# First mixer of a two-layer encoder trunk: k and v by features, recurrence laid between projection blocks, output projection in plain fp32

## The chip, the cores and the metric

The kernel runs on one core of a Trainium2 chip, as one launch. The metric is device microseconds of that launch. Engines are named as in the profile: PE is the matrix engine, DVE the vector engine, ACT the scalar engine, POOL is GpSimd, SP issues most of the DMAs. Each engine works through its own instructions in the order written; semaphores are the only links between them.

## What is computed

Two layers over 272 tokens (16 meta tokens and 256 real ones) of width 1024, all inputs fp32. The first layer's mixer, which the change rebuilds, is this, cut to what matters:

```python
def conv_gla_mixer(h, w_in, conv_w, wg_f, bg_f, wg_b, bg_b, gla_norm_w, w_out):
    u = h @ w_in
    a_b, a_c, a_x, q, k, v, r, g_f, g_b = jnp.split(u, splits, axis=-1)   # 512 x3, 256 x2, 512 x2, 16 x2
    y_a = a_b * centred_depthwise_conv3(a_c * a_x, conv_w)
    log_a_f = jax.nn.log_sigmoid((g_f @ wg_f + bg_f)) / GLA_GATE_TAU       # log_a_b likewise
    o_fwd = gla_chunked(qh, kh, vh, laf, True)                             # chunks of 64 tokens, 4 heads
    o_bwd = flip(gla_chunked(flip(qh), flip(kh), flip(vh), flip(lab), False))
    o = rms_norm per head (o_fwd + o_bwd) * gla_norm_w
    y_b = (o * jax.nn.silu(r))
    return jnp.concatenate([y_a, y_b], axis=-1) @ w_out

# gla_chunked, per chunk and head:
    scores = q*exp(cum) . k*exp(-cum), masked;  o_intra = scores @ v
    kv_chunk = (k*exp(cum_last - cum))^T @ v;  S = exp(cum_last) * S + kv_chunk;  o_inter = q*exp(cum) @ S_before
```

Behind the mixer stands a mixture of 32 experts with two chosen per token; then a second layer with grouped-query attention and experts of its own, then a final norm.

## The kernel before

Everything is written by hand, engine by engine, in one function; what the code says is the order, and no scheduler moves it. Three tiles hold the tokens: tile 0 has the 16 meta tokens, tiles 1 and 2 have 128 each (`TILE_AT`, `TILE_N`). `B[0]` to `B[7]` are the eight PSUM banks. `slots` are the 16 ring slots of 1 MB; the mixer's weights go through slots 0 to 7 (`MIX_RING`), and `scratch`, the mixer's working memory, lies over slots 8 to 15, so that expert weights can land there only when the mixer has done with it. The profile calls `scratch` whatever is carved out of it.

**Split products.** The mixer's projections are exact to fp32 by three products. A block `b` of 512 columns of weights comes in two units `u = 2b` and `2b+1`, for the features 0 to 3 and 4 to 7 of every eight. ACT rounds a unit into one of three buffers `mix_hi` (`round_mix`, L546); then DVE or POOL subtracts and writes the rest, `mix_lo`, in place (`low_mix`, L280; `MIX_POOL` says which units POOL takes). The features have the same two parts, `hnT_hi` and `hnT_lo`. PE then makes three passes for each product (`split_product`, L1331 to L1333): high by high, and twice high by low. Unit `u` can be rounded when unit `u-3` has been read; `mix_used` says that a block's first unit is read, `proj_ps` that a block's piece is finished. `feature_major` puts features on the rows and all 272 tokens in the columns; `token_major` puts a tile's tokens on the rows and 512 weight columns (256 for k) in the columns.

**Order on PE.** Gate ranks g; q feature-major, k token-major; the gate product (L1375); v token-major; six transposes that turn k (L1384); r token-major; conv block ax feature-major; the cumulated log decays (L1402) and end decays (L1410, L1411); conv blocks ac and ab. Then the recurrence: chunk sums (L1432, `chunk_sums`), scores (L1445), outputs from scores (L1460) and from states (L1473), transposes of the result yb (L1481), and the output projection, blocks 6 and 7, split and token-major, 144 passes. DVE does the decays, the conv taps (L913, L915), `ya` (L920), then the states: each of eight steps takes four pieces of 64 rows and 128 columns (L935, L937), then masks (L945), head norms (L958). The result becomes high and low parts again: ACT rounds ya (L611) and yb (L628), POOL and DVE write the low parts (L434, L964).

**Behind it.** DVE adds the projection to h (L990) tile by tile and norms tiles 0 and 1 in between (L816). PE transposes h (L1520) and makes the routing products. Experts go in quads: gather (L1608), gate and up products in four column strips of 32 rows (L1577), down (L1595), scatter (L1633). SP issues the expert weights: units 0 and 1 when block ac is read, 2 and 3 when ab is, 8 to 15 when yb is transposed and `pool_step` and `feat_hi` say that the scratch is free, 4 to 7 when the output weights are read (`first_units0`), and each further group of four when the stage that used its slots is done (`rest_of_units`). The second layer's projection back (L1798) is in plain fp32 with its features `hnT` and ring slots as they landed.

## Time and profile before

| | us |
|---|---|
| median of 3 runs | 828.09 (827.14 to 828.76) |
| the profiled execution | 826.41 |
| its span, first to last instruction | 824.6 |
| PE busy | 669.4 (81%) |
| DVE busy | 271.3 (33%) |
| ACT busy | 182.3 (22%) |
| POOL busy | 73.2 (9%) |
| bytes moved by DMA | 234.86 MB |

The profile is of one execution. A row of a line groups all instructions with that line, engine and shape: count, busy time together, mean time of one, and the engine's idle time before them with what ended it. On PE the mean is the time from start to end of one pass, and passes overlap; the rate is the stretch divided by the count. A plain fp32 product is recorded as two passes, a split product's passes as one each. PEclk is the granted clock as a share of 2.4 GHz: 1.00 or 0.50 at any moment, and a mean over a stretch.

### The profile page before, as it was taken

The numbers are of one execution on the slowest core, as the hardware profiler recorded it, in microseconds if no ns is written. First come the engines' busy times: TensorE is split into PE (matmuls) and PEld (weight loads), VectorE is DVE, ScalarE is ACT, GpSimd is POOL, SyncE is SP. The second block draws the span as 40 slices with busy tenths as digits, with TensorE's granted clock in tenths as the row PEclk, the third lists the DMA queues.
The fourth block names the chain that finished last, engine by engine and source line by source line (L and its number), as shares of the span: only waits on it lengthen the run. The fifth ranks groups of instructions, "written<-read, shape, count | busy, mean of one in ns | idle before, by whom it ended". The sixth has DMA issues, their size and how long they took to land.

```text
span 824.6 us, 9320 instructions
## 1 busy us (share of the span) xinstructions
PE 669.4 (81%) x3824; PEld 379.9 (46%) x3824; DVE 271.3 (33%) x608; ACT 182.3 (22%) x347; POOL 73.2 (9%) x47
## 2 busy tenths in 40 slices
PE   2999987896999679679678987899797668678665
PEld 2867986576727126226214665545535215215211
DVE  4242346335322212221214777612422202202204
ACT  4394513212101001000004426712111001001002
POOL 3223209300000000000004200000000000000000
PEclk9999997998999989979879999999799869869869
DMA  9534433783399999999998332059299999999991
GB/s 309 216 106 155 148 103 106 233 324 118 105 415 400 403 417 413 410 416 406 407 409 297 103 128 78 1 198 385 83 388 395 415 405 411 414 415 406 414 384 53
DMA packets 62164, 234.86 MB, mean 285 GB/s; under 512 B 6256, under 2 KB 6512, under 8 KB 53920
## 3 DMA queue, kind: packets, MB, share of 16 engines
q1 hardware_dynamic: 60848, 231.82, 72.5%
q0 software_dynamic: 1264, 2.34, 1.2%
q8 instruction: 34, 0.56, 0.3%
q14 instruction: 18, 0.15, 0.1%
HBM read 233.07 MB, written 1.05 MB: 284 GB/s over the span
## 4 chain that ended last, share of the span: by engine, by line
PE 50%; DMA 18%; SPq 13%; DVE 10%; ACT 5%; issue 3%; DVEq 0%; ACTq 0%
DMA ring<-in_moe_w_up 17%; SPq L329 13%; PE bank L1577 10%; PE bank L1608 7%; PE bank L1331 5%; PE bank L1332 5%; PE bank L1333 5%; PE bank L1633 4%; PE bank L1798 3%; PE bank L1595 3%; ACT scratch L759 2%; DVE mix_lo L280 1%; ACT mix_hi L546 1%; DVE scratch L1263 1%; DMA gain<-in_norm_mix 1%
## 5 line engine op out<-in xcount | busy, mean ns | idle before, releaser
L1577 PE MATMUL bank<-ring,hnT 128*32 128x512 f32 x1024 | 150.5, 743 | 83.5 <-DMA ring<-in_moe_w_up 80.0
L1577 PEld LDWEIGHTS bank<-ring,hnT 128*32 128x32 f32 x1024 | 38.4, 132 | 191.7 <-issue 119.1
L1608 PE MATMUL bank<-sel,hn 128*128 128x256 f32 x320 | 82.9, 419 | 0.3 <-DVE sel L1056 0.3
L1608 PEld LDWEIGHTS bank<-sel,hn 128*128 128x128 f32 x320 | 79.2, 336 | 3.5 <-issue 1.7
L280 POOL TENSOR_TENSOR mix_lo<-ring,mix_hi 128x2048 fp32r<-128x2048 f32 x11 | 51.9, 4727 | 315.4 <-ACT mix_hi L546 315.4
L1633 PE MATMUL bank<-moe_scratch 128*128 128x512 f32 (+1 forms) x160 | 78.1, 611 | 1.8 <-ACT moe_scratch L669 1.6
L1118 DVE TENSOR_TENSOR moe_scratch<-moe_scratch,bank 128x256 f32<-128x256 f32 x16 | 6.7, 421 | 215.9 <-ACT moe_scratch L663 215.9
L1331 PE MATMUL bank<-mix_hi,hnT_hi 128*128 128x512 f32 (+3 forms) x168 | 65.2, 388 | 3.9 <-DVE mix_lo L280 2.2
L1332 PE MATMUL bank<-mix_hi,hnT_lo 128*128 128x512 f32 (+3 forms) x168 | 64.8, 386 | 0.0
L1333 PE MATMUL bank<-mix_lo,hnT_hi 128*128 128x512 f32 (+3 forms) x168 | 64.6, 385 | 0.0
L1108 DVE TENSOR_TENSOR h<-bank,h 128x512 f32<-128x512 f32 (+1 forms) x80 | 55.1, 689 | 23.6 <-PE bank L1633 23.6
L1595 PE MATMUL bank<-ring,moe_scratch 128*32 128x512 f32 x512 | 58.2, 595 | 0.3 <-ACT moe_scratch L665 0.3
L663 ACT ACTIVATE moe_scratch<-bank 128x256 f32<-128x256 f32 x16 | 6.1, 383 | 216.2 <-PE bank L1577 216.2
L546 ACT ACTIVATE mix_hi<-ring 128x2048 fp32r<-128x2048 f32 x22 | 41.3, 1908 | 35.4 <-PE bank L1333 35.0
L1633 PEld LDWEIGHTS bank<-moe_scratch 128*128 128x128 f32 (+1 forms) x160 | 22.7, 169 | 55.3 <-issue 32.6
L280 DVE TENSOR_TENSOR mix_lo<-ring,mix_hi 128x2048 fp32r<-128x2048 f32 x11 | 27.8, 2539 | 30.7 <-ACT mix_hi L546 30.7
L1331 PEld LDWEIGHTS bank<-mix_hi,hnT_hi 128*128 128x128 f32 (+1 forms) x168 | 28.4, 169 | 17.8 <-issue 4.1
L1099 DVE COPY hnT<-bank 128x512 f32<-128x512 f32 x16 | 11.1, 692 | 76.6 <-PE bank L1608 76.6
L1331 PE MATMUL bank<-hnT_hi,mix_hi 128*128 128x272 f32 x112 | 32.7, 292 | 2.6 <-DVE mix_lo L280 1.8
L1333 PEld LDWEIGHTS bank<-mix_lo,hnT_hi 128*128 128x128 f32 (+1 forms) x168 | 28.2, 168 | 9.9 <-issue 0.6
L1332 PEld LDWEIGHTS bank<-mix_hi,hnT_lo 128*128 128x128 f32 (+1 forms) x168 | 28.4, 169 | 9.2 <-issue 0.8
L1332 PE MATMUL bank<-hnT_hi,mix_lo 128*128 128x272 f32 x112 | 32.3, 288 | 0.0
(262 smaller groups left out, 734.5 us busy)
## 6 DMA issues: line engine op xcount, KB each, us to landing
ring<-in_moe_w_gate SPq DMA_DIRECT2D x128, 512.0 KB, 14.3
ring<-in_moe_w_up SPq DMA_DIRECT2D x128, 512.0 KB, 14.5
ring<-in_moe_w_down SPq DMA_DIRECT2D x64, 1024.0 KB, 17.0
ring<-in_sc_w_in SPq DMA_DIRECT2D x12, 1024.0 KB, 12.5
ring<-in_att_w_in SPq DMA_DIRECT2D x6, 1024.0 KB, 15.3
ring<-in_sc_w_out SPq DMA_DIRECT2D x4, 1024.0 KB, 6.3
ring<-in_att_w_out SPq DMA_DIRECT2D x4, 1024.0 KB, 10.8
h<-in_x SPq DMA_DIRECT2D x2, 512.0 KB, 4.1
```

The lines of the kernel that those rows point to most:

```text
L280: ops.tensor_tensor(mix_lo[slot][:, :], slots[slot], mix_buf(u)[:, :].bitcast(f32), ALU.subtract)\
L329: sp.dma_start(gu[:, u], src).then_inc(sem(f"weights{l}_{stage_of(i) % 4}"), 16)
L546: nc.scalar.activation(mix_buf(u)[:, :], slots[at[-1]], ACT.Copy).then_inc(sem("mix_hi"), 1)
L1108: nc.vector.tensor_tensor(hh, B[[7, 4][k % 2]][0:n, :], hh, ALU.add).then_inc(sem(f"h_added{l}"), 1)
L1331: mm(dst, left[0], right[0], start=start, stop=False)
L1332: mm(dst, left[1], right[0], start=False, stop=False)
L1333: return mm(dst, left[0], right[1], start=False, stop=stop)
L1577: last = mm(B[2][at, :], xT[:, c, mine], w[j][:, :, cc, :], start=(c == 0), stop=(c == KC - 1))
L1595: last = mm(B[5 + half][at, :], heT[:, c, at], w[j][:, c * D + half * W:c * D + half * W + W], start=(c == 0), stop=(c == 1))
L1608: last = mm(B[k % 2][:, 2 * P * cc:2 * P * cc + 2 * P], hn[:, t, c:D:KC], picks, start=(t == a), stop=(t == b - 1))
L1633: mm(B[[7, 4][k % 2]][0:m, :], selgT[:, TILE_AT[t]:TILE_AT[t] + m], y[:, half, :], start=True, stop=True).then_inc(sem(f"sc_ps{l}"), 1)
L1798: last = mm(B[2 * half + i][:, :], hnT[:, c, i * P:(i + 1) * P], slots[u % MIX_RING][:, c % 4 * W:c % 4 * W + W], start=(c == 0), stop=(c ...
```

## The change

- **k and v** become feature-major. k's two blocks go straight to `kT`, and six transposes give the token-major `ktok`. v's four blocks go to `vT`, twelve transposes give `v`. Both lie in memory that `masked` takes later.
- **log decays**: ACT does Abs for three tiles, Exp for three, Ln for three, in place of all three functions for each tile in turn.
- **the last two pieces of a block** are made as a pair (`feature_pair`): first unit for both, then second unit for both.
- **order**: log and end decays come ahead of r; then one r tile, four chunk sums, the second r tile, four chunk sums, the third r tile, scores, ax, scores, ax pair, outputs, scores, ac, outputs, ac, outputs, ac pair, ab, yb transposes, ab pair, yb transposes.
- **states** are kept on 128 rows: a chunk sum makes four products of 64 rows each in place of two of 128, and DVE updates both heads of a pair in one instruction.
- **the output projection** is in plain fp32 from `hnT` and the ring slots: tiles 1 and 2 as whole products, the meta tile for both halves in four column strips whose sum a product with `sum4` takes. ya and yb are written to `hnT` directly. The units 12 to 15 are no longer rounded, and `sum4` is made ahead of the projection.

The diff, cut to its core:

```diff
-        MIX_POOL = [mix_unit(0, 0, 0) + u for u in range(2 * NMIX[0]) if u % 2 == 0 and u or u == 13] + [mix_unit(1, 0, 0) + u for u in range(3)]
+        MIX_POOL = [mix_unit(0, 0, 0) + u for u in range(2, 2 * NSPLIT[0], 2)] + [mix_unit(1, 0, 0) + u for u in range(3)]
...
                 sp.wait_ge(sem("ybT_ps"), 3)
-                sp.wait_ge(sem("pool_step"), 3)
-                sp.wait_ge(sem("feat_hi"), 1)
+                sp.wait_ge(sem("ya_ready"), 4)
...
+            def update_state(k):
+                d, i = k % 2, k // 2
+                j = i if d == 0 else 4 - i
+                dve.wait_ge(sem("kvs_ps"), k + 1)
+                got = B[SUM_BANK[k]][:, 0:2 * DV].rearrange("p (m n) -> p m n", m=2)
+                if i == 0:
+                    nc.vector.tensor_copy(state[:, 4 * d, :, :], got).then_inc(sem("state"), 1)
+                    return
+                dve.wait_ge(sem("state"), states_done(k - 2))
+                for m in range(2):
+                    nc.vector.scalar_tensor_tensor(state[:, 4 * d + i, m, :], state[:, 4 * d + i - 1, m, :], decay[:, 2 * d + m, j:j + 1], got[:, m, :],
+                                                   ALU.mult, ALU.add).then_inc(sem("state"), 1)
...
+            def feature_pair(w, pair, banks):
+                for half in range(2):
+                    for m, bank in zip(pair, banks):
+                        for c in range(4 * half, 4 * half + 4):
+                            last = split_product(bank[:, 0:T], w(c, m * P, (m + 1) * P), features(c, 0, T), c == 0, c == KC - 1)
+                        if half:
+                            last.then_inc(sem("proj_ps"), 1)
+                    if half == 0:
+                        last.then_inc(sem("mix_used"), 1)
...
                 for m in range(2):
-                    last = mm(bank[:, 256 * m:256 * m + 256], kend[p0:p0 + n, t, 256 * d + P * m:256 * d + P * (m + 1)],
-                              v[p0:p0 + n, t, 256 * m:256 * m + 256], start=True, stop=True)
+                    for hh in range(2):
+                        hd = 2 * m + hh
+                        last = mm(bank[64 * hh:64 * hh + 64, DV * m:DV * m + DV], kend[p0:p0 + n, t, 256 * d + DK * hd:256 * d + DK * hd + DK],
+                                  v[p0:p0 + n, t, DV * hd:DV * hd + DV], start=True, stop=True)
...
+            w = mix_weights(0, 3)
+            for m in range(2):
+                pe.wait_ge(sem("state"), states_done(4 + m))
+                feature_major(w, m, B[2 + m])
             scores(1, 2)
+            pe.wait_ge(sem("ax_ev"), 2)
+            feature_pair(w, (2, 3), (B[2], B[3]))
             outputs(0, 1)
             scores(2, 0)
...
+            w = mix_weights(0, 5)
+            for m in range(2):
+                pe.wait_ge(sem("z_ready"), m + 3)
+                feature_major(w, m, B[YA_BANK[m]])
...
+            def out_tile(half, t, bank):
+                pe.wait_ge(sem("ybT_ev"), t)
+                order = (4, 5, 6, 7, 0, 1, 2, 3)
+                for c in order:
+                    if c == 0:
+                        pe.wait_ge(sem("ya_ready"), 4)
+                    last = mm(bank[:, :], hnT[:, c, TILE_AT[t]:TILE_AT[t] + P], out_weights(half, c), start=(c == 4), stop=(c == 3))
+                last.then_inc(sem("proj_ps"), 1)
+            def out_meta(half, bank):
+                pe.wait_ge(sem("ybT_ev"), 3)
+                for g in (1, 0):
+                    for j in range(4):
+                        last = mm(bank[32 * j:32 * j + 32, :], hnT[:, 4 * g + j, 0:32], out_weights(half, 4 * g + j), start=(g == 1), stop=(g == 0))
+                last.then_inc(sem("proj_ps"), 1)
...
+            out_tile(0, 1, B[7])
+            out_tile(0, 2, B[4])
+            out_meta(0, B[0])
+            out_meta(1, B[3])
+            out_meta_sum(0, B[5])
+            out_tile(1, 1, B[6])
+            out_meta_sum(1, B[1])
+            out_tile(1, 2, B[2])
```

How it moves instructions, at three places. Here a full fp32 product is one row, and a split product three. On PE in the recurrence, before: chunk sums (L1432), scores (L1445), outputs (L1460, L1473) in one piece.

```order
L1432 MATMUL bank<-hn,scratch 128x256 x12
L1445 MATMUL bank<-scratch 128x128 x8
L1432 MATMUL bank<-hn,scratch 128x256 x4
L1445 MATMUL bank<-scratch 128x128 x8
L1460 MATMUL bank<-hn,scratch 128x128 x8
L1473 MATMUL bank<-scratch 64x128 x16
L1445 MATMUL bank<-scratch 16x16 x8
L1460 MATMUL bank<-hn,scratch 128x128 x8
```

The same place in the changed kernel (L1483 and L1494 are the outputs, L1468 the scores, L1346 to L1348 a split product), the end of the ax pair and the start of ac:

```order
L1346 MATMUL bank<-hnT_hi,mix_hi 128x272
L1347 MATMUL bank<-hnT_hi,mix_lo 128x272
L1348 MATMUL bank<-hnT_lo,mix_hi 128x272
L1483 MATMUL bank<-hn,scratch 128x128 x8
L1494 MATMUL bank<-scratch 64x128 x16
L1468 MATMUL bank<-scratch 16x16 x8
L1346 MATMUL bank<-hnT_hi,mix_hi 128x272
L1347 MATMUL bank<-hnT_hi,mix_lo 128x272
```

The first outputs and the meta tile's scores stand between 96 split passes of ax and 24 of ac's first piece. On DVE around the states, before (L906 is the conv product, L913 and L915 the taps, L920 ya, L935 and L937 the states, L945 the masks):

```order
L906 TENSOR_TENSOR scratch<-bank,scratch 128x272
L913 TENSOR_SCALAR scratch<-scratch,conv_w 128x272 x4
L915 SCALAR_TENSOR_TENSOR scratch<-scratch,conv_w 128x272 x8
L920 TENSOR_TENSOR scratch<-bank,scratch 128x272 x4
L935 COPY scratch<-bank 64x128 x8
L937 SCALAR_TENSOR_TENSOR scratch<-scratch,bank 64x128 x24
L945 TENSOR_TENSOR scratch<-bank,consts 128x256 x8
```

And now (L911 and L915 are the states, L929 and L930 the decayed q and k, L922 the gain on r, L282 a low part, L945 the masks):

```order
L911 COPY scratch<-bank 128x256 x2
L915 SCALAR_TENSOR_TENSOR scratch<-scratch,bank 128x128 x4
L929 TENSOR_TENSOR scratch<-scratch 128x544
L930 TENSOR_TENSOR scratch<-scratch 128x544
L929 TENSOR_TENSOR scratch<-scratch 128x544
L930 TENSOR_TENSOR scratch<-scratch 128x544
L922 TENSOR_TENSOR hn<-hn,gla_gain 16x512
L922 TENSOR_TENSOR hn<-hn,gla_gain 128x512
L915 SCALAR_TENSOR_TENSOR scratch<-scratch,bank 128x128 x8
L282 TENSOR_TENSOR mix_lo<-ring,mix_hi 128x2048
L922 TENSOR_TENSOR hn<-hn,gla_gain 128x512
L945 TENSOR_TENSOR scratch<-bank,consts 128x256 x8
```

The states now stand ahead of the conv products, in 14 instructions in place of 32, and a low part stands between them and the masks. On PE at the output projection, before:

```order
L1481 MATMUL bank<-consts,scratch 128x16 x4
L1331 MATMUL bank<-mix_hi,hnT_hi 16x512
L1332 MATMUL bank<-mix_hi,hnT_lo 16x512
L1333 MATMUL bank<-mix_lo,hnT_hi 16x512
L1331 MATMUL bank<-mix_hi,hnT_hi 16x512
```

And now, the whole of it (L1555 full tiles, L1562 meta tile, L1568 its sum):

```order
L1502 MATMUL bank<-consts,scratch 128x16 x4
L1555 MATMUL bank<-ring,hnT 128x512 x16
L1562 MATMUL bank<-ring,hnT 32x512 x16
L1568 MATMUL bank<-moe_scratch,sum 16x512
L1555 MATMUL bank<-ring,hnT 128x512 x8
L1568 MATMUL bank<-moe_scratch,sum 16x512
L1555 MATMUL bank<-ring,hnT 128x512 x8
```

144 single passes became 50 plain products, and the meta tile went from the first place of each half to the middle.

## Rows read from the trace of the kernel before

**Rows 1.** The page, second section: the span in 40 slices of 20.6 us.

```profile
GB/s 309 216 106 155 148 103 106 233 324 118 105 415 400 403 417 413 410 416 406 407 409 297 103 128 78 1 198 385 83 388 395 415 405 411 414 415 406 414 384 53
```

**Rows 2.** Stages of the first mixer and behind it; stretch, its length, then per engine.

```profile
core 0: us, PE busy (x) PEld busy (x) DVE busy (x) ACT busy (x) POOL busy (x), PEclk, DMA share, GB/s
25.50:40.30 14.80, 14.80 (x124) 14.08 (x121) 1.19 (x3) 2.44 (x4) 4.81 (x1) 1.00 0.47 172
40.30:43.20 2.90, 2.90 (x8) 0.81 (x8) 2.21 (x2) 2.90 (x3) 0.37 (x1) 1.00 0.53 145
43.20:59.90 16.70, 16.70 (x73) 11.17 (x72) 5.15 (x9) 15.59 (x18) 4.57 (x1) 1.00 0.27 101
59.90:78.20 18.30, 18.30 (x85) 12.74 (x85) 3.96 (x4) 7.80 (x9) 4.61 (x1) 1.00 0.33 115
78.20:96.70 18.50, 18.08 (x128) 16.30 (x127) 5.82 (x9) 10.06 (x18) 4.60 (x1) 1.00 0.63 210
96.70:123.90 27.20, 24.97 (x196) 24.34 (x194) 13.54 (x29) 6.36 (x5) 5.26 (x1) 1.00 0.27 91
123.90:155.10 31.20, 22.91 (x205) 18.12 (x204) 20.19 (x68) 12.37 (x35) 25.37 (x19) 0.84 0.39 101
155.10:190.20 35.10, 35.10 (x145) 22.96 (x145) 9.59 (x15) 4.72 (x8) 0.00 (x0) 0.95 0.78 299
190.20:218.80 28.60, 21.51 (x154) 17.43 (x153) 13.69 (x61) 5.31 (x11) 0.53 (x1) 0.82 0.28 93
218.80:420.00 201.20, 165.48 (x947) 77.10 (x947) 46.32 (x71) 15.01 (x29) 0.00 (x0) 0.92 1.02 404
```

**Rows 3.** The DMA queue's issues in order of time: start, length.

```profile
218.82 0.33 SPq L329 DMA_DIRECT2D ring<-in_moe_w_gate  x1
```

**Rows 4.** PE groups by line and shape, 20 to 191 us: count | busy, mean ns.

```profile
L1331 PE MATMUL bank<-hnT_hi,mix_hi 128*128 128x272 f32 x112 | 32.7, 292 | 2.6 <-DVE mix_lo L280 1.8 <-DVE scratch L920 0.8
...
L1331 PE MATMUL bank<-mix_hi,hnT_hi 128*16 128x512 f32 x32 | 13.2, 412 | 0.9 <-DVE hnT_lo L964 0.9
```

**Rows 5.** Plain fp32 products: the second layer's projection by shape, and gate products in time.

```profile
L1798 PE MATMUL bank<-ring,hnT 128*128 128x512 f32 x64 | 27.7, 594 | 0.5 <-ACT hnT L772 0.5
...
215.13 3.64 PE L1577 MATMUL bank<-ring,hnT 128*32 128x512 f32 x32 [0.83 <-issue]
```

**Rows 6.** Groups by line and shape up to 216 us: rounding and low parts.

```profile
L546 ACT ACTIVATE mix_hi<-ring 128x2048 fp32r<-128x2048 f32 x16 | 30.1, 1909 | 35.1 <-PE bank L1333 35.0
...
L280 DVE TENSOR_TENSOR mix_lo<-ring,mix_hi 128x2048 fp32r<-128x2048 f32 x8 | 18.3, 2292 | 27.3 <-ACT mix_hi L546 27.3
...
L280 POOL TENSOR_TENSOR mix_lo<-ring,mix_hi 128x2048 fp32r<-128x2048 f32 x8 | 38.2, 4782 | 72.5 <-ACT mix_hi L546 72.5
```

**Rows 7.** Recurrence in order of time: start, length, engine, what, count, idle before.

```profile
123.83 4.04 PE L1432 MATMUL bank<-hn,scratch 16*128 16x256 f32 x24
...
125.00 2.53 DVE L935 COPY scratch<-bank 64x128 f32<-64x128 f32 x8 [0.61 <-PE bank L1432]
...
127.56 6.02 DVE L937 SCALAR_TENSOR_TENSOR scratch<-scratch,bank 64x128 f32<-64x128 f32 x16
...
130.61 1.52 PE L1445 MATMUL bank<-scratch 64*128 64x128 f32 x16 [2.74 <-DVE scratch L937]
...
142.92 1.17 PE L1473 MATMUL bank<-scratch 64*64 64x128 f32 x32
```

**Rows 8.** The two stretches of low granted clock in the mixer; columns as in rows 2.

```profile
131.40:141.70 10.30, 8.27 (x38) 6.42 (x36) 7.73 (x22) 0.00 (x0) 10.30 (x4) 0.50 0.02 6
155.20:158.80 3.60, 3.60 (x10) 1.21 (x10) 0.69 (x2) 0.00 (x0) 0.00 (x0) 0.53 0.92 330
```

**Rows 9.** The six transposes of k, by their line.

```profile
L1384 PE MATMUL bank<-consts,scratch x6: 230/272/328, 60.0 to 60.8; 128*128 128x128 f32 x4, 16*128 16x16 f32 x2
```

**Rows 10.** DVE's add to h and its norm in order of time.

```profile
184.71 0.69 DVE L990 TENSOR_TENSOR h<-bank,h 128x512 f32<-128x512 f32 x1 [1.73 <-PE bank L1333]
...
187.23 1.28 DVE L816 SCALAR_TENSOR_TENSOR hn<-h,stats,gain 128x1024 f32<-128x1024 f32 x1
```

More of the change, by code:

```diff
@@ L939, in mask_scores @@
+            dve.wait_ge(sem("gla_params_in"), 128)
+            gate_scaled(0)
+            gate_scaled(1)
+            for k in range(4, 8):
+                update_state(k)
+            low_mix(dve, nc.vector, 0, 7)
+            gate_scaled(2)
             def mask_scores(i, t):
@@ L1354, in product, with feature_major @@
                 last.then_inc(sem("proj_ps"), 1)
-            def feature_major(w, m, bank, closing=False):
-                product(bank[:, 0:T], lambda c: (w(c, m * P, (m + 1) * P), features(c, 0, T)), closing)
+            def feature_major(w, m, bank):
+                product(bank[:, 0:T], lambda c: (w(c, m * P, (m + 1) * P), features(c, 0, T)), False)
+            def feature_pair(w, pair, banks):
+                for half in range(2):
+                    for m, bank in zip(pair, banks):
[5 more added lines that the diff above has]
+                        last.then_inc(sem("mix_used"), 1)
             def token_major(w, t, lo, hi, bank, rows=None, closing=False, at=None):
@@ L1366, in _ @@
             w = mix_weights(0, 0)
[L1367 to L1370 removed]
+            feature_major(w, 0, B[3])
             pe.wait_ge(sem("g_ev"), 1)
@@ new lines, in _ @@
+            pe.wait_ge(sem("q_ev"), 1)
+            feature_major(w, 1, B[3])
+            pe.wait_ge(sem("kT_ev"), 2)
+            for t in (1, 2):
+                for m in range(2):
+                    last = nc.tensor.transpose(B[6][:, 256 * (t - 1) + P * m:256 * (t - 1) + P * (m + 1)], kT[:, m, TILE_AT[t]:TILE_AT[t] + P], ident)
+            last.then_inc(sem("kT_ps"), 1)
+            pe.wait_ge(sem("vT_ev"), 1)
+            for m in range(2):
+                last = nc.tensor.transpose(B[7][0:NM, P * m:P * (m + 1)], kT[:, m, 0:NM], ident)
@@ L1423, in _ @@
-            pe.wait_ge(sem("v_ev"), 3)
+                for m in range(4):
+                    last = nc.tensor.transpose(B[3 + t][0:n, m * P:(m + 1) * P], vT[:, m, TILE_AT[t]:TILE_AT[t] + n], ident)
+                last.then_inc(sem("vtok_ps"), 1)
+            pe.wait_ge(sem("k_ev"), 2)
+            log_decays(3)
+            for t in range(3):
+                n = TILE_N[t]
+                pe.wait_ge(sem("v_ev"), t + 1)
+                mm(B[3 + t][0:n, 0:256], strict_bwd[0:n, 0:n], la[0:n, t, 0:256], start=True, stop=True)
+                mm(B[3 + t][0:n, 256:512], strict_fwd[0:n, 0:n], la[0:n, t, 256:512], start=True, stop=True).then_inc(sem("kend_ps"), 1)
@@ L1482, in yb_transposes @@
                 last.then_inc(sem("ybT_ps"), 1)
-            for k in range(6):
+            w = mix_weights(0, 2)
+            token_major(w, 0, 0, W, B[R_BANK[0]])
+            pe.wait_ge(sem("kend"), 6)
+            pe.wait_ge(sem("E_exp"), 6)
+            for k in range(4):
                 chunk_sums(k)
-            pe.wait_ge(sem("state"), 16)
+            token_major(w, 1, 0, W, B[R_BANK[1]])
+            for k in range(4, 8):
+                chunk_sums(k)
+            token_major(w, 2, 0, W, B[R_BANK[2]], closing=True)
@@ new lines, in out_meta_sum @@
+            def out_meta_sum(half, bank):
+                pe.wait_ge(sem("parts"), half + 1)
+                pe.wait_ge(sem("w_route"), 4)
+                mm(bank[0:NM, :], sum4[:, :], y[:, half, :], start=True, stop=True).then_inc(sem("out_meta"), 1)
+            out_tile(0, 1, B[7])
[6 more added lines that the diff above has]
+            out_tile(1, 2, B[2])
```

385 lines of the change are left out of this document (176 added, 209 removed).

## The prediction

> **What bounds the kernel now.** The page's second section comes first: DMA throughput lies near 400 GB/s in two long stretches, the two expert layers, and at 100 to 300 GB/s ahead of each [rows 1]. The stage table says the same by time: from 218.8 to 420 us the DMA share is 1.02 and PE is busy for 165 of 201 us, so that the first expert layer runs at the speed of its weights [rows 2]. That stream starts at 218.82 us, when the first quad's first half is done and its four slots come free [rows 3]; until then only the 16 units that fit the ring can be fetched. Everything behind 218.8 us hangs on that moment. So a us taken out of the first mixer is a us off the end, as long as the 16 units are there in time, and nothing that the change does behind this point counts.
>
> Within the mixer I read the stage table by PE [rows 2]. From 25.5 to 123.9 us PE is busy in nearly all of the 98.4 us: the projections are bound by PE itself. From 123.9 to 155.1 us, 31.2 us, it is the recurrence: PE has 22.9 us of busy time, part of it at a granted clock of 0.50 [rows 8], and waits on DVE's state updates and masks in between [rows 7]. From 155.1 to 190.2 us the output projection fills PE. Then come 28.6 us of norm, routing, gathers and the first gate products, which the change hardly touches. The edit can therefore gain in three ways: fewer PE passes, PE work laid under the recurrence's waits, and a cheaper output projection.
>
> **Rates.** 120 passes of q and k take 14.8 us, so 0.123 us for one of 272 or 256 columns; 72 passes of v take 16.7 us, 0.232 us for one of 512 columns, also where the tile has only 16 rows [rows 2, 4]. A plain fp32 product of 128x512 is two passes: 64 of them take 27.7 us, 0.43 us each [rows 5].
>
> **k and v feature-major.** k: 48 passes instead of 72, 5.9 us instead of 8.8. v: 4 blocks of 24 passes of 272 columns, 11.8 us instead of 16.7; the 16 meta tokens no longer cost a whole tile. The six k transposes stay (1.1 us); twelve v transposes are new. Six transposes lie between 60.0 and 61.1 us [rows 9], 0.18 each, so +2.1 us. Net gain 5.7 us.
>
> **Recurrence.** Chunk sums: before 32 passes of 256 columns, 24 of them in 4.0 us at full clock [rows 7], 0.16 us each; now 64 of 128 columns, each for 64 of the output rows. Bounds: 0.036 us each as in the state products, whose 32 passes take 1.17 us in four corners of the array [rows 7], so 2.3 us; and the old rate per column, 0.08 us each, so 5.4 us. I take two products side by side: a full pass of 512 columns is 0.43 us [rows 5], so one of 128 is 0.107 and half of that 0.053, 3.4 us; it lies between, nearer the row that also splits the output rows. State updates: before 8 copies and 24 multiply-adds on 64 rows (2.5 and about 9 us of DVE [rows 7]); now 2 copies of 256 columns and 12 multiply-adds of 128 columns on 128 rows, by the same per-instruction time about 5.4 us. In the walk below no PE instruction waits for them. Scores: 16 passes in 1.5 us at full clock [rows 7], twice, and 0.6 for the meta tile, 3.6 us. Outputs: about 3.1 us for each full tile and 2.4 for the small one, 8.6 us; yb transposes 2.1 us. Together 17.7 us of PE work in place of a 31.2 us stretch.
>
> **PE's total to the output projection.** From 25.5 us: q 5.9, k 5.9, gates 2.9, v 11.8, transposes 3.2, log decays and end decays 6.3 (18.5 us of the stage 78.2 to 96.7 less 11.8 for ax and 0.4 idle [rows 2]), r 16.7, ax, ac and ab 35.4, recurrence 17.7: 105.8 us. Before, the same list was 93.8 us of projections and decays, 4.6 us of waits, and 31.2.
>
> **Waits that the new order leaves.** All engines are in order, so I walked the new code with the durations of the trace: rounding on ACT 1.91 us, low part 2.29 us on DVE or 4.8 us on POOL [rows 6], evictions of a whole bank 0.69 us [rows 10], smaller ones less. The three high buffers decide when a unit can be rounded: unit u needs unit u-3 read. The walk gives, as low part ready / first needed: u3 41.8 / 42.0 us, u4 50.9 / 61.8, u5 55.0 / 63.3, u6 69.7 / 83.6, u7 83.4 / 85.1, u8 97 / 101, u9 98.5 / 102.3, u10 110 / 118, u11 119.8 / 119.9. None is late, three by a hair, so each us lost on ACT ahead of u3, u7 or u11 goes through. The pair of blocks that closes each weight block frees the first half 3 us before its end where the old order left 1.5 us, which is what makes these fit. Queued behind u11's low part on DVE is the product for the third conv block, and the first ab block needs its bank: it waits 1.9 us. Score head 3 waits 0.4 us for the silu of the last r tile, which stands on ACT behind u7. The projection waits 0.5 us for ACT's yb copies, which may only start when all reads of the old features are done. Sum 2.8 us. The conv taps and ya products run under the pair of ab blocks and the first 3.4 us of the projection. If that cover failed they would cost at most their 6 us. So the projection starts at 25.5 + 105.8 + 2.8 = 134.1 us, against 155.1: 21.0 us earlier.
>
> **Output projection.** Two full tiles, two halves, 8 chunks are 32 products, 64 passes, as in the second layer's projection: 27.7 us [rows 5]. For these tiles alone that is dearer than the 96 single passes of 0.232 us (22.3 us). The meta tile pays it back: before 48 passes, 11.1 us; now 32 passes in four column strips, 3.6 us by the gate products, which are the same form [rows 5], and two summing products, 1.7 us. 33.0 us against 35.1, of which 3.6 us had been at clock 0.53 [rows 8]: gain 2.1 us. Four roundings, four low parts and POOL's feature low part go away, but they lay beside PE.
>
> **Behind it.** The meta half is now added to h after the third of four full tiles, 6.8 us before the end, and each add with its norm takes DVE 3.8 us (184.71 to 188.5 [rows 10]); two of them end 0.8 us after the last product, so the last add starts 0.8 us late. I charge 0.7 us. The weights: units 8 to 15 can be issued at about 135 us, 4 and 5 at about 150, 6 and 7 at 167. Twelve units of 1 MB at 400 GB/s are 31 us, so all are in by about 175, against 196 us for the first stage's end: covered with 20 us to spare. The earlier ones take the place of the same transfers before.
>
> **A rule about the clock.** Rows: the granted clock fell to 0.50 from 131.4 to 141.7 us, when PE had just waited for DVE, and again at 155.2 us after a stretch of transposes and waits [rows 8]; around the six k transposes at 60 us, with full products before and behind, it stayed at 1.00 [rows 2, 9]. The new order puts twelve more transposes between log decays at 56 us, and lays dense blocks where the waits were, so I count no low clock there. The Trainium skill (TensorE: Matmul & The Clock Gate, Part 4: PE-mode transpose) says that transposes do not count as busy for the gate; by it the new run of transposes could let the clock fall where the sum has it full. No row here separates the two, and the third rival below prices it from rows.
>
> **Sum.** 21.0 + 2.1 - 0.7 = 22.4 us. The profiled execution of 826.4 us (span 824.6) would become 804.0 (span 802.2); the median of 828.1 lies 1.7 above that execution, so 805.7 us.
>
> **Rivals.**
> 1. The waits come back in the new order. ACT stands in order at each recurrence step; a late square or silu delays the next rounding. Three of the nine units have under 2 us of slack. If two block heads each wait a full rounding and low part, 4.2 us [rows 6], and the sums keep the old rate (+2.0), the gain is 22.4 - 10.4 = 12.0: about 816. With only one of the two, 810 to 814. For it: the slack; against it: the idle time of ACT and DVE in the stage table, over half of most stages.
> 2. The other side: slower. The fp32 projection runs at half clock. It needs 33 us of PE at full clock and comes after a break for yb. At clock 0.5 passes take twice as long, as they did from 155.2 to 158.8 us [rows 8]. It decides from about two thirds of the projection: 22.4 us lost; over the whole, +33, so 839. Against it: in the second layer the same 64 passes ran at 0.43 us throughout, after a wait too [rows 5].
> 3. One low stretch. The clock falls once for 3.4 to 10.3 us, as it did twice [rows 8], in the interleaved part: half of that is lost, 2 to 5 us, so 808 to 811. This is also where the transposes rule would lead.
> 4. It does not carry: the time to 218.8 is gained but the weights are late. Then the time stays at 828. Against it the 20 us to spare above.
> 5. Better than the walk: sums at 2.3 us, no head waits, the routing stretch with less low clock (its PE clock is 0.82 [rows 2], worth, as an estimate, up to 2.5 us): 800 to 802.
>
> **Chances.** Forecast, 803 to 809: 0.55. One low stretch or part of rival 1, 809 to 814: 0.2. Rival 1 whole, up to 818: 0.08. Rival 5: 0.12. Rival 4: 0.02. Rival 2: 0.03. For 8 in 10 the range takes the forecast, the part of rival 5 down to 800 and the cases up to 815. Faster 0.95, within 0.2% (1.7 us, about what this kernel's measurement can tell) 0.02, slower 0.03.
>
> **What would show it.** Output projection starting near 134 us with its first pass on the ring's weights; 64 passes in 27 to 28 us and the strips in under 4; the first stream issue near 196 us and an unbroken 400 GB/s behind it; v and k at 0.123 us a pass; sums of eight passes in 0.43 us. Wrong if PE idles more than 5 us between 25 and 134 us, if the clock row shows a fall there, or if the stretch from the projection's end to the first stream issue differs from 28.6 us by more than 2.

## The result, and the profile after

The changed kernel took 808.22 us (median of 4 runs, 805.51 to 810.31) beside 828.42 us of the kernel before: ratio 0.9754, 95% interval 0.972 to 0.9787. In two later comparisons of the same two kernels the ratios were 0.9727 (0.9686 to 0.9768) and 0.9733 (0.971 to 0.9756), with medians of 806.17 and 806.12 us. The forecast of 805.7 us against 828.1 is a ratio of 0.973. The profiled execution took 807.99 us with a span of 806.2 us.

The page's DMA row answers [rows 1]: the first long stretch near 400 GB/s starts earlier by one slice.

```profile
GB/s 302 234 165 46 107 128 214 402 245 63 383 404 415 407 408 415 416 405 416 409 387 89 184 131 1 2 365 262 160 417 407 400 418 403 412 415 409 409 344 53
```

The stage table of the changed kernel, columns as in [rows 2]: length, busy time of PE, PE loads, DVE, ACT, POOL, PE clock, DMA share, GB/s. The first row runs from the first mixer product to the output projection; the next two are stretches inside it.

```profile
25.80:135.57 109.77, 107.69 (x851) 94.50 (x848) 44.68 (x98) 44.25 (x77) 32.96 (x20) 0.98 0.40 129
32.90:36.30 3.40, 3.40 (x18) 3.40 (x17) 0.00 (x0) 2.84 (x4) 0.00 (x0) 0.51 0.00 0
55.61:63.60 7.99, 7.99 (x50) 6.30 (x50) 4.11 (x7) 5.41 (x12) 0.00 (x0) 1.00 0.76 264
135.57:169.10 33.53, 33.53 (x101) 13.25 (x102) 8.20 (x20) 4.55 (x11) 0.00 (x0) 1.00 0.98 375
169.10:198.17 29.07, 22.02 (x153) 17.69 (x153) 13.48 (x59) 5.23 (x11) 0.53 (x1) 0.82 0.27 92
198.17:399.40 201.23, 165.39 (x947) 77.03 (x947) 46.35 (x71) 15.01 (x29) 0.00 (x0) 0.93 1.02 404
```

Before, 129.6 us lay between 25.5 and the projection; now it is 109.8, with PE busy for 107.7 of them. The half clock behind 123.9 us is gone, and so is the one at the projection's start [rows 8], but a new one stands at 32.90 us, far ahead of the interleaved part. The rest follows at the old speed.

PE and the DMA queue in order of time (start, length, engine, what, count, idle before it): the chunk sums, the first ab block, the v transposes, the first product of the output projection, the first issue of the stream. They answer [rows 7], [rows 9] and [rows 3].

```profile
58.40 1.47 PE L1433 MATMUL bank<-consts,scratch 128*16 128x128 f32 x12
69.22 1.70 PE L1452 MATMUL bank<-hn,scratch 16*64 16x128 f32 x32
76.60 1.59 PE L1452 MATMUL bank<-hn,scratch 64*64 64x128 f32 x32
121.74 0.39 PE L1346 MATMUL bank<-hnT_hi,mix_hi 128*128 128x272 f32 x1 [1.75 <-DVE scratch L964]
135.57 1.99 PE L1555 MATMUL bank<-ring,hnT 128*128 128x512 f32 x4 [0.34 <-ACT hnT L646]
198.17 0.33 SPq L340 DMA_DIRECT2D ring<-in_moe_w_gate  x1
```

What was 31.2 us of steps and waits has become short pieces between dense blocks. The only waits left are 1.75 and 0.34 us. The stream's issue moved from 218.82 to 198.17 us, 20.65 earlier. The span, however, is only 18.4 us shorter. Part of the difference stands in the last rows of the chain of waits (start, length, what), first of the kernel before, then of the changed one:

```profile
817.28 1.23 ACT hn L501 x3
818.83 1.28 DVE hn L816
```

```profile
797.56 1.23 ACT hn L505 x3
799.21 1.05 issue
800.46 1.28 DVE hn L828
```

A wait of 1.05 us that no engine causes has come in ahead of the last norm, in code that the diff doesn't touch. From the start of ACT's last rows to DVE's norm it is 2.90 us in place of 1.55, so 1.35 us of the end lie there. Three things were open: how much the interleaving is worth and through what, what the new output projection is worth, and where the half clock and this last wait come from.

### The profile page after: what moved, and what is told of

The parts are those of the page before. It is cut to its first block, busy times and chain, and to the rows that moved or that the text cites. A ratio compares the mean times of both kernels' runs of the same rounds, so it can differ in the third digit from the quotient of the medians.

```text
span 806.2 us, 9290 instructions
## 1 busy us (share of the span) xinstructions
PE 655.8 (81%) x3824; PEld 367.4 (46%) x3824; DVE 262.2 (33%) x590; ACT 168.9 (21%) x338; POOL 56.6 (7%) x43
## 3 DMA queue, kind: packets, MB, share of 16 engines
HBM read 233.07 MB, written 1.05 MB: 290 GB/s over the span
## 4 chain that ended last, share of the span: by engine, by line
PE 55%; DMA 19%; SPq 13%; DVE 6%; ACT 4%; issue 3%; DVEq 0%; ACTq 0%
DMA ring<-in_moe_w_up 18%; SPq L340 13%; PE bank L1649 10%; PE bank L1680 7%; PE bank L1346 5%; PE bank L1347 5%; PE bank L1348 5%; PE bank L1705 4%; PE bank L1555 3%; PE bank L1869 3%; PE bank L1667 3%; ACT scratch L771 2%; DVE scratch L1278 1%; DVE att_rcp L1264 1%; DVE hn L828 1%
## 5 line engine op out<-in xcount | busy, mean ns | idle before, releaser
L282 POOL TENSOR_TENSOR mix_lo<-ring,mix_hi 128x2048 fp32r<-128x2048 f32 x8 | 37.7, 4715 | 324.4 <-ACT mix_hi L550 324.4
L1346 PE MATMUL bank<-hnT_hi,mix_hi 128*128 128x272 f32 x160 | 47.7, 298 | 1.7 <-DVE scratch L964 1.7
L1705 PEld LDWEIGHTS bank<-moe_scratch 128*128 128x128 f32 (+1 forms) x160 | 22.8, 169 | 55.7 <-issue 32.9
L1347 PE MATMUL bank<-hnT_hi,mix_lo 128*128 128x272 f32 x160 | 46.8, 293 | 0.0
L1348 PE MATMUL bank<-hnT_lo,mix_hi 128*128 128x272 f32 x160 | 46.7, 292 | 0.0
L550 ACT ACTIVATE mix_hi<-ring 128x2048 fp32r<-128x2048 f32 x18 | 34.1, 1911 | 14.3 <-PE bank L1348 13.6
L282 DVE TENSOR_TENSOR mix_lo<-ring,mix_hi 128x2048 fp32r<-128x2048 f32 x10 | 25.7, 2577 | 34.0 <-ACT mix_hi L550 34.0
L1346 PE MATMUL bank<-mix_hi,hnT_hi 128*128 128x512 f32 (+1 forms) x72 | 29.9, 415 | 3.5 <-DVE mix_lo L282 2.2
L1346 PEld LDWEIGHTS bank<-hnT_hi,mix_hi 128*128 128x128 f32 x160 | 30.9, 193 | 3.6 <-DVE scratch L964 2.0
L1348 PEld LDWEIGHTS bank<-hnT_lo,mix_hi 128*128 128x128 f32 x160 | 30.8, 193 | 0.0
L1347 PEld LDWEIGHTS bank<-hnT_hi,mix_lo 128*128 128x128 f32 x160 | 30.8, 193 | 0.0
L1347 PE MATMUL bank<-mix_hi,hnT_lo 128*128 128x512 f32 (+1 forms) x72 | 29.1, 404 | 0.0
```

Source lines behind the costliest of these rows:

```text
L282: ops.tensor_tensor(mix_lo[slot][:, :], slots[slot], mix_buf(u)[:, :].bitcast(f32), ALU.subtract)\
L550: nc.scalar.activation(mix_buf(u)[:, :], slots[at[-1]], ACT.Copy).then_inc(sem("mix_hi"), 1)
L1346: mm(dst, left[0], right[0], start=start, stop=False)
L1347: mm(dst, left[1], right[0], start=False, stop=False)
L1348: return mm(dst, left[0], right[1], start=False, stop=stop)
L1705: mm(B[[7, 4][k % 2]][0:m, :], selgT[:, TILE_AT[t]:TILE_AT[t] + m], y[:, half, :], start=True, stop=True).then_inc(sem(f"sc_ps{l}"), 1)
```

## Experiments

### The interleaving

The weight blocks keep their places and columns, but the steps of the recurrence from the scores on stand behind them, as in the kernel before:

```diff
@@ TensorE
-            scores(0, 1)
             ...
-            scores(1, 2)
             ...
-            outputs(0, 1)
-            scores(2, 0)
             ...
-            outputs(1, 2)
             ...
-            outputs(2, 0)
             ...
+            feature_pair(w, (2, 3), (B[YA_BANK[2]], B[YA_BANK[3]]))
+            pe.wait_ge(sem("qk_dec"), 4)
+            pe.wait_ge(sem("ya_ready"), 4)
+            scores(0, 1)
+            scores(1, 2)
+            outputs(0, 1)
+            scores(2, 0)
+            outputs(1, 2)
+            outputs(2, 0)
```

ACT and DVE take their parts in the new order too. PE now waits for DVE's ya products ahead of the scores, since one of the scores' banks holds a part of ya.

> The changed kernel with scores, outputs, head norms and yb transposes behind the conv blocks again (chunk sums stay between the r tiles; nothing is left out). The PE work is the same, so what differs is only the cover. Theory 1 (a good part of the gain is that the conv blocks lie under the recurrence's waits): the masks, squares, roots and head norms stand bare, 4 to 8 us more than the changed kernel, 812 to 816 us. Theory 2 (the gain is fewer passes, the order gives little): within 1.5 us of the changed kernel. Theory 3 (the order gives nearly all that the recurrence lost): 12 us or more.

It took 817.79 us (815.26 to 819.82), ratio 0.9864 (0.9817 to 0.991), 11.6 us more than the changed kernel in the same comparison (806.17):

> The changed kernel once more, as the base for the others of this call. Both theories: ratio to before 0.974 to 0.977, projection start (first plain pass of the output projection) near 135.6 us, first stream issue near 198.2 us. The trace of the changed kernel showed a granted clock of 0.51 from 32.9 to 36.3 us, behind the three gate products. If that fall belongs to the order it is here again; if it is chance it is gone or elsewhere, and the projection starts about 1.5 us earlier.

The stage tables, of the variant and then of the changed kernel in that comparison, and the variant's waiting PE rows:

```profile
28.35:62.70 34.35, 34.35 (x230) 30.28 (x229) 12.80 (x18) 20.62 (x31) 7.08 (x2) 0.95 0.47 166
62.70:111.90 49.20, 45.67 (x329) 38.05 (x327) 19.31 (x36) 17.81 (x17) 22.56 (x17) 1.00 0.32 96
111.90:127.40 15.50, 13.80 (x97) 13.62 (x97) 6.52 (x17) 0.00 (x0) 0.66 (x2) 0.89 0.60 181
127.40:143.84 16.44, 13.78 (x172) 11.60 (x173) 8.09 (x33) 5.96 (x29) 0.00 (x0) 0.90 0.37 120
143.84:179.07 35.23, 35.23 (x102) 13.90 (x102) 6.71 (x15) 4.21 (x10) 0.00 (x0) 0.95 0.77 298
```

```profile
27.86:60.70 32.84, 32.84 (x230) 28.76 (x229) 12.80 (x18) 20.50 (x31) 7.43 (x2) 1.00 0.51 180
60.70:118.89 58.19, 56.44 (x490) 47.76 (x488) 25.98 (x66) 22.60 (x43) 23.19 (x18) 1.00 0.28 82
118.89:134.25 15.36, 15.02 (x108) 14.78 (x108) 5.52 (x15) 0.65 (x2) 0.00 (x0) 0.89 0.50 170
134.25:167.78 33.53, 33.52 (x101) 13.25 (x102) 8.20 (x20) 4.55 (x11) 0.00 (x0) 1.00 0.98 374
```

```profile
127.40 2.90 PE L1469 MATMUL bank<-scratch 64*128 64x128 f32 x32 [1.69 <-issue]
137.38 1.92 PE L1484 MATMUL bank<-hn,scratch 16*16 16x128 f32 x16 [0.64 <-DVE scratch L946]
143.31 0.60 PE L1503 MATMUL bank<-consts,scratch 16*128 16x16 f32 x4 [2.02 <-DVE scratch L959]
```

From the gate products to the projection the variant needs 115.5 us, the changed kernel 106.4. PE's idle time in it is 7.9 us against 2.1, so waits make 5.8 of the 9.1 us; 1.69 of them are the wait at 127.40 us, by the code the one for ya, whose products DVE ends at 127.3. The other 3.3 us are busy time, and most of that is clock. This execution of the variant has three stretches of half clock: from 31.2 to 34.7 us, from 113.2 to 116.6 and from 140.5 to 147.3. Each of the three profiles of the changed kernel has one, at the place of the first or of the second. So of the variant's first two, one (1.7 us) may be chance. The third has no counterpart there. It began ahead of the wait of 2.02 us for yb, when PE had made small products for 13 us with waits of 1.69 and 0.64 us, and it went on into the projection:

```profile
140.40:141.29 0.89, 0.89 (x5) 0.49 (x4) 0.00 (x0) 0.83 (x6) 0.00 (x0) 0.53 0.00 0
143.84:147.30 3.46, 3.46 (x5) 1.51 (x5) 0.69 (x4) 0.22 (x1) 0.00 (x0) 0.50 0.63 213
```

It costs 0.7 us ahead of the projection and 1.7 us in it: 35.23 us at 0.95 against 33.53 at 1.00, with the same products in both. What remains of the 3.3 us, 0.9, the clock doesn't explain. The expectation of 4 to 8 us priced waits alone, and these are 5.8. The difference at the stream's first issue, 11.25 us in these two profiles, is these waits, 2.4 us of half clock that comes with the order, 1.7 that may be chance, the 0.9, and 0.5 us ahead of the gate products.

### The output projection

The kernel before, with the fp32 output projection and its strips for the meta rows as the only change:

```diff
-            for half in range(2):
-                w = mix_weights(0, 6 + half)
-                for t in range(3):
-                    token_major(w, t, 0, W, B[2 + 3 * half + t], closing=t == 2)
+            out_tile(0, 1, B[2])
+            out_tile(0, 2, B[3])
+            out_meta(0, B[5])
+            out_meta(1, B[7])
+            out_meta_sum(0, B[1])
+            out_tile(1, 1, B[6])
+            out_meta_sum(1, B[0])
+            out_tile(1, 2, B[4])
```

> The kernel before with only the output projection changed: plain fp32, meta tile in four column strips, units 12 to 15 not rounded, yb's low part gone. Theory 1 (my sum): 33.5 us for the projection against 35.1, of which 1.8 are the low clock at its start; 0.9 us less ahead of it, 0.7 us more behind it: 1 to 3 us faster than before, 825 to 827 us. Rival A (plain passes are dearer and the strips do not pay it back): 3 to 5 us slower. Rival B (rounding and low parts of units 12 to 15 on ACT, DVE and POOL held the recurrence up): 4 us or more faster.

829.45 us (825.3 to 833.53), ratio 1.0001 (0.9974 to 1.0028): no gain that the times show. The interval reaches from 2.2 us faster to 2.3 us slower, so that the forecast's 2.1 us is just inside it and the stages have to decide. Its stage table, the projection and the stretch to the stream's first issue, and PE's rows around the projection's start:

```profile
154.34:189.47 35.13, 35.13 (x103) 13.74 (x101) 6.80 (x16) 4.22 (x10) 0.00 (x0) 0.95 0.77 299
189.47:218.54 29.07, 22.03 (x154) 17.70 (x153) 13.55 (x59) 5.24 (x11) 0.53 (x1) 0.82 0.27 92
```

```profile
153.99 0.42 PE L1463 MATMUL bank<-consts,scratch 16*128 16x16 f32 x4 [2.07 <-DVE scratch L951]
154.34 4.23 PE L1493 MATMUL bank<-ring,hnT 128*128 128x512 f32 x6
```

The projection starts 0.8 us earlier than in the kernel before, since there is no low part of yb to wait for, but it lasts 35.13 us in place of 35.1 [rows 2]. Its first six passes take 4.23 us in place of 2.6, behind a wait of 2.07 us: the clock fell 1.3 us into the projection, to 0.51 from 155.6 to 159.0 us, as the three-pass form had run at 0.53 there [rows 8]. At full clock both forms take the same time: the fp32 form 33.53 us in the changed kernel, the three-pass form 35.1 less about half of its 3.6 us at low clock, so 33.4. The forecast had compared 33.0 us at full clock with 35.1 of which 3.6 were slow. The tail is 0.4 us longer, and the issue comes 0.3 us earlier. So 2.1 us was no gain of the form. What the changed kernel does gain there, 1.6 us, it gets from the interleaving, which put dense blocks ahead of the projection where a wait had been: without it the same fp32 form took 35.23 us, as the variant above shows.

### Chunk sums over all 128 rows or on two halves

The states go back to 64 rows: per step two products of 256 columns on all output rows in place of four of 128 columns on half of them.

```diff
-                    for hh in range(2):
-                        hd = 2 * m + hh
-                        last = mm(bank[64 * hh:64 * hh + 64, DV * m:DV * m + DV], kend[...DK * hd...],
-                                  v[...DV * hd...], start=True, stop=True)
+                    last = mm(bank[:, 256 * m:256 * m + 256], kend[...P * m...],
+                              v[...256 * m...], start=True, stop=True)
```

> The changed kernel with the states as before: chunk sums as two products of 256 columns, states updated in four pieces of 64 rows. Theory 1 (DVE has room there, only PE's time for the sums counts): sums take 5.1 us instead of 3.3, the 5 us more on DVE are covered or cost up to 1, in all 1 to 3 us slower than the changed kernel. Rival (the shorter chain of state updates on DVE is what makes the new order fit): the low part of unit 7 and the masks come late, 5 us or more slower.

808.71 us (806.87 to 809.37), ratio 0.9748 (0.9708 to 0.9789), 2.5 us more than the changed kernel in the same comparison. Its sums in order of time:

```profile
68.47 3.06 PE L1454 MATMUL bank<-hn,scratch 16*128 16x256 f32 x16
77.21 2.96 PE L1454 MATMUL bank<-hn,scratch 64*128 64x256 f32 x16
```

6.02 us in place of 3.29 (5.1 had been expected), 2.7 us of PE time. From the gate products to the projection it is 109.1 us in place of 106.4, so there is no new wait: the time moves by what PE does. The 18 additional DVE instructions for the updates cost nothing, they lie under the blocks. Two passes side by side, each on half of the output rows, take 0.051 us each for 128 columns (64 in 3.29 us); the estimate was 0.053.

### The wait at the first ab block

DVE's rows in the changed kernel ahead of that block (start, length, engine, what, count, idle before):

```profile
119.04 2.29 DVE L282 TENSOR_TENSOR mix_lo<-ring,mix_hi 128x2048 fp32r<-128x2048 f32 x1 [1.82 <-ACT mix_hi L550]
121.25 0.78 DVE L964 TENSOR_TENSOR scratch<-bank,scratch 128x272 f32<-128x272 f32 x2
```

```diff
-            low_mix(dve, nc.vector, 0, 11)
             conv_input(2)
+            low_mix(dve, nc.vector, 0, 11)
             conv_input(3)
```

> DVE takes the input of the last conv stage ahead of the low part of unit 11. Theory 1 (the block ab0 waits 1.75 us only since its input stands on DVE behind that low part of 2.3 us, which itself waited for ACT): the wait goes, ab0 starts some 1.7 us earlier, the low part starts as before or up to 0.8 us later and is still in time for the block that reads it, and the projection starts 1.2 to 1.7 us earlier. Theory 2 (the low part is late as well): the wait moves to the first block that reads it, and nothing is gained. 805 to 807 us under theory 1, 806 to 808 under theory 2.

```profile
116.73 0.44 DVE L964 TENSOR_TENSOR scratch<-bank,scratch 128x272 f32<-128x272 f32 x1 [1.33 <-PE bank L1348]
117.24 2.29 DVE L282 TENSOR_TENSOR mix_lo<-ring,mix_hi 128x2048 fp32r<-128x2048 f32 x1
```

```profile
28.92:63.30 34.38, 34.38 (x236) 29.42 (x236) 14.24 (x22) 21.86 (x33) 6.24 (x2) 1.00 0.45 159
63.30:117.80 54.50, 54.50 (x481) 46.92 (x480) 22.85 (x62) 21.26 (x42) 21.67 (x16) 1.00 0.29 85
117.80:131.91 14.11, 13.77 (x112) 13.42 (x110) 7.31 (x16) 0.65 (x2) 1.53 (x3) 1.00 0.63 198
```

The wait is gone and nothing took its place. From the gate products to the projection it is 103.0 us against 106.4: 1.75 for the wait and 1.65 since this execution had no half clock there. The median, 806.68 us (801.99 to 807.5), does not show it against 806.12.

### Where the half clock stands

The changed kernel again, and the gate products one piece later, behind q's second piece:

> The changed kernel once more, beside its variants. Its profiles so far show a stretch of half clock at another place each: one ran at clock 0.51 from 32.9 to 36.3 us behind the gate products, the other at full clock there and at 0.89 over the blocks from 118.9 to 134.3 us. If the place is a matter of the execution, this profile shows one of the two again, or none; the first stream issue comes at 196 to 198.5 us. 806 to 808 us.

```diff
             feature_major(w, 0, B[3])
+            feature_major(w, 1, B[4])
             pe.wait_ge(sem("g_ev"), 1)
             ...
-            feature_major(w, 1, B[4])
```

> The three pairs of gate products (33 rows deep, 2.94 us) go one feature-major piece later, behind q's second piece. Theory 1 (the fall to half clock at 33 us comes from the gate products): no half clock between 30 and 36 us in this profile; if one comes, it comes behind the products in their new place, some 5 us later. Theory 2 (it comes from what stands at that time whatever is there): half clock again between 31 and 36 us. Theory 3 (neither; no half clock anywhere before the recurrence): full clock to 60 us. A stretch that goes is worth 1.4 to 1.7 us, one that only moves nothing, so 805 to 808 us.

The changed kernel in the last comparison had its half clock at 31 to 35 us, as in its first profile; the one between them had none there and a stretch of 3.4 us from 119.0 us on instead, right behind the wait at the first ab block. The variant took 805.47 us (804.72 to 807.64) and shows, in PE's order of time and in its stage table:

```profile
30.82 3.07 PE L1399 MATMUL bank<-scratch 33*16 33x512 f32 x6
```

```profile
33.30:36.70 3.40, 3.40 (x14) 2.89 (x13) 0.00 (x0) 2.98 (x5) 0.00 (x0) 0.53 0.01 2
```

Theory 3 is out. This profile alone doesn't decide between the other two: against the two profiles with the fall the products moved by 1.6 and 2.4 us, the fall by 0.6 and 2.1, so that it again stands at their end, but also within 31 to 36. The eleven profiles of the changed kernel and its variants say more: in eight of them the clock falls here, each time between 0.4 us ahead of the end of the gate products and 0.8 us behind it. With the products in their first place it falls at 31.2 to 33.0 us (four profiles), with them later at 33.5 to 35.7 us (four profiles). So it is tied to them, as theory 1 has it. But they don't suffice: they ran without it in the kernel before (from 40.3 us), in the second profile of the changed kernel, in the variant with the conv input first and in the one with 14 clears below. What decides from one execution to the next stays open. Ahead of the products the clock rises to full speed at 23.3 to 26.3 us, and they start at 27.9 to 32.2 us, so that the two lie differently to each other each time; no run varies that alone. The stretch is worth 1.65 us.

### The wait that no engine causes

All edits together (both above, and the meta rows' second sum one tile earlier):

> Both of these edits, and the meta rows' sum of the output projection's second half one product tile earlier. The three gains together if they are real: 1.5 us of clock where a stretch goes, 1.7 us of the wait at ab0, 0.4 to 0.8 us less behind the projection; so 803 to 805 us, against 806 to 808 of the changed kernel. If the clock stretch only moves: 804 to 806.

805.77 us (805.01 to 806.53), ratio 0.9725 (0.9706 to 0.9744), with the stream's first issue 1.8 us earlier than the changed kernel's in the same comparison (197.03):

```profile
195.21 0.33 SPq L340 DMA_DIRECT2D ring<-in_moe_w_gate  x1
```

Against the changed kernel's 806.12 us this is no difference that the measurement can tell, and no variant is faster than the changed kernel by one. The earlier meta sum gave nothing: the last add to h starts 0.1 us behind the last product in place of 0.5, but the stretch behind the projection is no shorter. It takes 29.5 us at a clock of 0.77, and 29.2 with 14 clears (below) at 0.82; without this edit it is 29.2 with the conv input first at 0.77, and 28.6 to 29.2 in the changed kernel at 0.82. The DVE's waits without a releaser (what, total, times, longest), in this kernel:

```profile
DVE scratch L1164 <- issue: 3.3, 1, 3.3
DVE stats L816 <- issue: 1.3, 1, 1.3
```

Both stand where DVE comes out of a skipped loop over further expert rounds, one behind each expert layer; at the second place two small instructions run ahead of the wait in this kernel. The kernel before has 0.9 us at the first and none at the second, the variant with 64-row states the same (its DVE program is 18 instructions longer, not shorter as the expectation below has it), and the one with only the output projection 2.8 us at the second. To tell place from time, clears of one column of a free tile were put at DVE's start, where it idles:

```diff
+            for k in range(14):   # 14, 30, 46
+                nc.vector.memset(sum4[32 * (k // 16):32 * (k // 16) + 32, k % 16:k % 16 + 1], 0.0)
             norm(0)
```

> e_best with 14 one-column clears of a free tile (DVE, in its idle time of the first 8 us) ahead of everything else, so that each later DVE instruction stands 14 places further on in its program. It is about a wait that no engine causes: 'issue', DVE, 1.1 to 1.5 us ahead of the last norm and 3.2 us behind the first MoE's skipped loop in every kernel with the changed kernel's DVE program; before and the variant with 18 DVE instructions fewer show 0 and 0.9 us there. Theory 1 (the wait hangs on where in the program the instructions behind a skipped loop stand): some of the paddings of 14, 30 and 46 show 0 and 0.9 us, others 1 to 3 us, and the end follows by that much. Theory 2 (it hangs on what happens in time, not on the place): 1.1 to 1.5 and 3.2 us in all three. Span 802 to 804 us where the wait goes, 803 to 805 us where it stays.

> The same with 30 clears. Theory 1: a different pair of waits than with 14 or 46 in at least one of the two places. Theory 2: 1.1 to 1.5 us ahead of the last norm and 3.2 us behind the skipped loop, as in e_best.

> The same with 46 clears. Theory 1: a different pair of waits than with 14 or 30 in at least one of the two places. Theory 2: 1.1 to 1.5 us ahead of the last norm and 3.2 us behind the skipped loop, as in e_best.

With 14 clears, then with 46 (with 30 it is as with 46), the same view and the end of the chain:

```profile
DVE stats L808 <- issue: 2.6, 1, 2.6
DVE scratch L1166 <- issue: 0.9, 1, 0.9
```

```profile
DVE scratch L1166 <- issue: 0.9, 1, 0.9
```

```profile
797.18 1.24 ACT hn L505 x3
798.73 1.28 DVE hn L828
```

Theory 1 holds for the waits: nothing but the place of the instructions in DVE's program changed, and the second wait is 1.3, 2.6, 0 and 0 us with 0, 14, 30 and 46 clears, the first 3.3, 0.9, 0.9 and 0.9. The number of DVE instructions on the pages sorts all thirteen profiles: with 590 (the changed kernel and its variants, seven profiles) the waits are 3.1 to 3.3 and 1.3 to 1.5 us, with 604 (14 clears, and the kernel before with the new output projection) 0.9 and 2.6 to 2.8, with 608, 620 and 636 they are 0.9 and nothing.

The DMA view has what is waited for. Queue 14, of the kind "instruction", moves pieces of 8 KB. From the last add to h to 1 us behind the wait it moves two of them where the wait is long and one where it is not, at both places and in all thirteen profiles. At the second place, in the changed kernel (797.4 to 801.5 us) and with 46 clears (797.0 to 799.7 us; packets, MB, share of the DMA engines):

```profile
q14 instruction: 2, 0.02, 1.3%
```

```profile
q14 instruction: 1, 0.01, 1.2%
```

So the long wait goes with one more piece of code to load. That the piece is DVE's is an inference, since the queue's rows name no engine.

From the last add to the last norm it is 1.7 us without the second wait and 3.0 to 3.4 with it. That the end follows, as theory 1 also had it, is not seen: the times are 805.6, 806.46 and 805.51 us, of two runs each, and from the stream's first issue to the end the spans of all kernels here take 605.8 to 609.6 us, where the 609.6 is one without the wait.

## Why the prediction was right, step by step

**The stream sets the end: right.** 20.65 us earlier at the first issue, and the stage behind it has the same DMA share of 1.02. Rival 4 (the weights are late) did not come up; rival 1 neither, with 2.1 us of idle PE up to the projection, nor rival 2, with the projection at full clock.

**PE's work: right to 0.3 us.** 105.8 us were summed. Measured were 107.69 us busy, of which 1.65 are the slow stretch, so 106.0. Within it the chunk sums took 3.3 us (3.4 expected) and the twelve v transposes 1.47 (2.1 expected: taken at 0.18 each from the six of k, they took 0.12). The passes of 272 columns ran at 0.124 us (100 of them from 36.4 to 48.8 us). That k and v by features are worth 5.7 us rests on this rate and the counts; no run takes them out alone.

**Waits: right, a little high.** 2.8 us expected, 2.1 found: 1.75 at ab0 (1.9), 0.34 for yb (0.5), none for score head 3 (0.4). That the first one stands behind the low part of unit 11 is what moving it showed.

**The start of the projection: 134.1 us expected, 135.57 found.** The mixer's first product came 0.3 us later, the slow stretch added 1.65, the waits gave 0.7 back and PE's work took 0.2. The sum had counted no low clock. One of the forecast's own signs of being wrong, a fall of the clock between 25 and 134 us, came with it. This is rival 3 in small: one stretch, but at 32.9 us instead of in the interleaved part, and 1.65 us instead of 2 to 5. The Trainium skill's rule on transposes (TensorE: Matmul & The Clock Gate, Part 4: PE-mode transpose) did not lead there: the stretch from 55.6 to 63.6 us, with 24 passes of decay products and the twelve transposes, ran at 1.00, and the fall came 16 us ahead of the first transpose of k. That section is about the transpose mode. No run shows whether these transposes use it, and 1.47 us of them between other products is no hard test of the rule.

**The output projection: the wrong reason.** The term of 2.1 us failed. Its row of before held 1.7 us of half clock, and the term charged this to the three-pass form. The form alone brought nothing (829.45 us, and 35.13 us for the stage); at full clock it takes 33.5 us to about 33.4. The gain of 1.6 us in the changed kernel is real, but belongs to the interleaving, which the sum had priced by waits and passes only. That the total is right within 0.5 us on this term is luck.

**The tail: right.** 29.07 us behind the projection against 28.6, so 0.5 for the 0.7 charged.

**Behind the stream: not foreseen.** "Nothing counts there" holds for work, not for the place of code: up to 2.2 us of the span came back there, 1.35 of it by the wait ahead of the last norm. The rest is within the 3.8 us by which this stretch differs between these kernels.

So the first issue came 2.2, 0.3 and 1.0 us later than the forecast's 196 in the three profiles of the changed kernel, and the time 2.5, 0.5 and 0.4 us above 805.7.

## What to carry to other kernels

Lay dense blocks between the steps of a dependent chain even if the waits that they fill are short: here 5.8 us of waits went, and with them at least 2.4 us of half clock; by the medians the order is worth 11.6 us. When a stage is compared across forms, take both at the same clock; the half clock in the projection's row belonged to what stood ahead of it, not to the instructions in it. A difference of 1 to 3 us in code that the diff doesn't touch, with "issue" as its cause behind a skipped loop, can be a matter of where the code lies: look for a transfer of the instruction queue beside it.

## What the runs showed of the hardware that was not expected

- DVE waits behind a skipped loop for 0.9 or 3.1 to 3.3 us at one place and for 0, 1.3 to 1.5 or 2.6 to 2.8 us at another, by nothing but the number of instructions ahead in its program. Each long wait has one transfer of 8 KB on the instruction queue more than the short ones.
- A 128x512 product in plain fp32 (two passes, 0.43 us each) and three passes on split operands with 0.232 us each cost 0.87 and 0.70 us a product; the strips for the 16-row tile (32 passes in 3.64 us) make up for just that.
- Twice the clock fell by half where PE had had small products and short waits: 0.9 us ahead of a wait of 2.02 us (at 140.4 us, order put back), and 1.3 us into the projection behind one of 2.07 us (at 155.6 us, output projection alone). It cost 1.7 us of the projection each time. It also comes without any wait, at the end of three products (six passes) that use 33 of the 128 rows, in eight profiles of eleven.
